# A two-block transformer kernel: order of copies and modulation blocks in the first block, who makes three low parts, and when late modulation weights are taken

## The chip, the cores and the metric

One core of a Trainium2 chip runs the whole program as one launch. The metric is device time in microseconds (us); lower is better. The kernel before took 1699.9 us, the median of 3 runs (1697.79 to 1700.61). The engines are TensorE (PE: matrix products and transposes; PEld is its weight load), VectorE (DVE), ScalarE (ACT), GpSimd (POOL) and SyncE (SP), which issues nearly all DMAs.

## The reference, cut to what matters

256 tokens of width 1024 go through a first block (a mixed attention, then a product-key expert layer) and a second block of two layers (NSA attention and MLP, then sliding-window attention with sinks and MLP). The parts that the change touches:

```python
# first block, attention
proj = h @ w_in                      # queries, keys, values, index queries/keys
ik_n = rms(ik)                       # index keys
score = sum_h(w_idx * relu(q_idx @ ik_n.T)); idx = top_k(score, 64)
x = x + g1 * (y @ w_out)             # out projection of the first block: "out1"
# experts
q = h @ w_query                      # "wq"
s = q @ sub_keys.T; i_top = top_k(s, 16)
x = x + g2 * experts(...)
# second block, two layers i = 0, 1
mod = silu(c) @ ada_w[i] + ada_b[i]  # six vectors sh1, sc1, g1, sh2, sc2, g2
y = (nsa if i == 0 else swa)(modulate(rms(x), sh1, sc1)) @ w_out   # "out2", "out3"
x = x + (1 + g1) * rms(y)
y = relu(modulate(rms(x), sh2, sc2) @ w_up)**2 @ w_down            # "mlp2", "mlp3"
x = x + (1 + g2) * rms(y)
```

## The kernel before, in words

All weight matrices are cut into chunks of 128 x 1024 float32 (512 KB) and laid out in one stream, in the order of use: `qk1` (18 chunks), `v1` (8), `out1` (8), `wq` (16), `subkeys`, `u` and `v` (128 each), `nsa`, `phi`, `out2` (8), `mlp2` (64), `swa` (10), `out3` (8), `mlp3` (64). SP loads them into a ring of 8 slots; chunk c is loaded once chunk c - 8 has been used.

Each product is made exact in three passes (`passes`, L665 to L671): a weight is split into a high part (ACT copies it to `weights_high`, L1238, 4 buffers) and a low part, weight minus high (`weights_low`, written over the ring slot). Low parts are made by POOL (`lows`, L627) or by DVE (`low`, L1711); the table `BY_DVE` says which chunk is whose. For `out1` and `out3` all are POOL's, for `out2` the first four are DVE's. The first two chunks of `wq`, `nsa`, `mlp2`, `swa` and `mlp3` are pairs with buffers of their own (`pair_high` L1242, `pair_low` L1716).

Modulation vectors are made on DVE, block by block: `ada_block` (L1662) multiplies a 128 x 1024 piece of modulation weights by the broadcast condition and sums over its columns. 144 such pieces are loaded by SP beside the stream.

Every engine runs one program written out by hand, with semaphores between them; no scheduler chooses an order. The places of the change, in order of time:

- First block, index scores: after all 18 `qk1` chunks PE transposes the index keys (L921), waits until ACT has copied them, and makes the index scores (L930), which DVE turns into a top-64 mask; then come the `v1` chunks. ACT makes the high part of the last `qk1` chunk's successor before it copies that chunk's result (`take`).
- Values: after `v1` ACT makes a high part, then copies both token tiles out of PSUM (L1397), and only then can attention use these banks (scores L801 and L811).
- First attention: 8 steps. PE: scores, transposes (L834), values (L856). ACT: exponentials, copies. DVE: maxima, scaling, low parts of y (L1791), and after each step's scaling one modulation block in steps 0 to 3 and two in steps 4 to 7; 4 more follow before `out1` ends.
- `wq` and sub-keys: PE waits for all 16 copies of `wq` results, then starts the sub-key products (L953).
- `out2` and `mlp2`: DVE takes modulation blocks 0 to 3 of the last 32, then the pair's low parts, then the residual (L2190), the norm (L1700) and so on. SP loads blocks 0 to 5 ahead; in `mlp2` DVE takes block j + 4 in step j.
- `swa`, third attention, `out3`: DVE rotates keys and queries (L2130 to L2132) while POOL makes the low parts of `out3`'s first four chunks.

Between a block's residual and its next product, PE transposes the normed tiles (L730), with `keep_busy` products (L748) between the two tiles.

## Time and profile before

| | |
|---|---|
| median of 3 runs | 1699.9 us |
| the profiled execution | 1700.1 us |
| its span in the profile | 1698.3 us |
| PE, DVE, ACT, POOL busy | 96%, 72%, 53%, 27% |
| granted TensorE clock, mean | 0.987 of full speed |
| weights moved | 344 MB, 203 GB/s |

The profile is one execution. Of the time, 1.8 us lie outside the span. "Busy" of PE is near its whole span, so what can be saved without taking work away is the little time in which it waits or runs at the lower clock.

### The profile page before, as it was taken

What the parts mean: (1) busy time and instruction counts of PE and PEld (TensorE: products, weight loads), DVE (VectorE), ACT (ScalarE), POOL (GpSimd) and SP (SyncE); (2) the same over time, 40 slices, a digit from 0 to 9 for tenths busy, and PEclk for the clock granted to TensorE, in tenths of its full rate; (3) what the DMA queues carried; (4) which work ended last, traced back from release to release, by engine and by line L of the source; (5) the groups of instructions that cost most, each with busy time, mean ns of one, the idle gap of its engine ahead of it and who ended that gap; (6) DMA issues with size and microseconds to landing.
All of it is one profiled execution on the core that took longest, in us unless ns stands there. A gap on an engine that the chain in (4) does not pass through costs nothing.

```text
span 1698.3 us, 31246 instructions
## 1 busy us (share of the span) xinstructions
PE 1635.0 (96%) x10735; PEld 1440.5 (85%) x10740; DVE 1222.5 (72%) x2382; ACT 908.2 (53%) x1747; POOL 450.5 (27%) x181
## 2 busy tenths in 40 slices
PE   6988999999999999999999999988999999799998
PEld 3975899999999999788888888965799998489997
DVE  4468869589718894877778777746598877666665
ACT  3445554455459995554554545267544445564443
POOL 0970238989875556000000000000200001020000
PEclk9999999999999999999999999999999999899999
DMA  9877776555553334888888776430488766146563
GB/s 342 303 186 238 263 231 182 184 182 178 185 173 112 113 114 134 287 285 287 285 293 295 286 258 181 152 147 1 152 298 288 275 203 159 38 150 187 186 188 106
DMA packets 105527, 344.25 MB, mean 203 GB/s; under 512 B 18484, under 2 KB 22340, under 8 KB 105445
## 3 DMA queue, kind: packets, MB, share of 16 engines
q1 hardware_dynamic: 101092, 339.19, 60.1%
q10 hardware_dynamic: 4352, 4.02, 0.8%
q8 instruction: 46, 0.75, 0.2%
q14 instruction: 37, 0.30, 0.1%
HBM read 341.02 MB, written 1.10 MB: 201 GB/s over the span
## 4 chain that ended last, share of the span: by engine, by line
PE 81%; issue 5%; POOL 4%; DVE 4%; ACT 3%; DMA 1%; ACTq 1%; SPq 0%; DVEq 0%; POOLq 0%
PE banks L669 23%; PE banks L670 23%; PE banks L671 23%; POOL weights_low L627 4%; PE banks L975 3%; PE banks L834 1%; PE banks L801 1%; PE banks L850 1%; DMA ring<-in_stream 1%; DMA arena<-in_ada 1%; ACT arena L1292 1%; PE banks L702 1%; PE banks L703 1%; PE banks L706 1%; DVE arena L2132 0%
## 5 line engine op out<-in xcount | busy, mean ns | idle before, releaser
L1238 ACT ACTIVATE weights_high<-ring 128x1024 fp32r<-128x1024 f32 x470 | 494.7, 1053 | 336.0 <-PE banks L671 324.9
L627 POOL TENSOR_TENSOR weights_low<-ring,weights_high 128x1024 fp32r<-128x1024 f32 x176 | 449.3, 2567 | 666.4 <-ACT weights_high L1238 666.1
L669 PE MATMUL banks<-ht_high,weights_high 128*128 128x256 f32 x1936 | 556.7, 288 | 3.9 <-DVE ht_low L1739 3.9
L670 PE MATMUL banks<-ht_low,weights_high 128*128 128x256 f32 x1936 | 547.8, 283 | 0.0
L671 PE MATMUL banks<-ht_high,weights_low 128*128 128x256 f32 x1936 | 547.7, 283 | 0.0
L1711 DVE TENSOR_TENSOR weights_low<-ring,weights_high 128x1024 fp32r<-128x1024 f32 x294 | 358.4, 1223 | 130.0 <-ACT weights_high L1238 129.0
L669 PEld LDWEIGHTS banks<-ht_high,weights_high 128*128 128x128 f32 x1936 | 371.1, 192 | 7.2 <-issue 4.0
L670 PEld LDWEIGHTS banks<-ht_low,weights_high 128*128 128x128 f32 x1936 | 371.4, 192 | 2.6
L671 PEld LDWEIGHTS banks<-ht_high,weights_low 128*128 128x128 f32 x1936 | 371.1, 192 | 0.0
L1662 DVE SCALAR_TENSOR_TENSOR arena<-arena,cs 128x1024 f32<-128x1024 f32 x80 | 110.1, 1386 | 47.7 <-DMA arena<-in_ada 42.8
L669 PE MATMUL banks<-weights_high,ga_parts 128*128 128x512 f32 x256 | 99.9, 390 | 2.8 <-DVE ga_parts L2039 2.8
L647 POOL MEMSET arena<- 128x1144 f32 x1 | 1.1, 1056 | 381.4 <-PE banks L671 381.4
L669 PE MATMUL banks<-weights_high,hidden_high 128*128 128x512 f32 x256 | 100.3, 392 | 0.0
L670 PE MATMUL banks<-weights_low,hidden_high 128*128 128x512 f32 x256 | 100.3, 392 | 0.0
L671 PE MATMUL banks<-weights_high,ga_parts 128*128 128x512 f32 x256 | 99.6, 389 | 0.0
L670 PE MATMUL banks<-weights_low,ga_parts 128*128 128x512 f32 x256 | 99.6, 389 | 0.0
L669 PE MATMUL banks<-weights_high,ga_more 128*128 128x512 f32 x256 | 99.6, 389 | 0.0
L670 PE MATMUL banks<-weights_low,ga_more 128*128 128x512 f32 x256 | 99.6, 389 | 0.0
L671 PE MATMUL banks<-weights_high,ga_more 128*128 128x512 f32 x256 | 99.6, 389 | 0.0
L671 PE MATMUL banks<-weights_high,hidden_low 128*128 128x512 f32 x256 | 99.6, 389 | 0.0
L2000 DVE TENSOR_TENSOR arena<-arena,banks 128x512 f32<-128x512 f32 (+1 forms) x64 | 44.0, 688 | 61.0 <-PE banks L975 55.6
L1593 ACT ACTIVATE arena<-banks 128x256 f32<-128x256 f32 x64 | 24.6, 385 | 111.5 <-PE banks L671 109.0
(274 smaller groups left out, 2589.8 us busy)
## 6 DMA issues: line engine op xcount, KB each, us to landing
ring<-in_stream SPq DMA_DIRECT2D x490, 512.0 KB, 3.5
arena<-in_ada SPq DMA_DIRECT2D x88, 512.0 KB, 5.5
ada_ring<-in_ada SPq DMA_DIRECT2D x56, 512.0 KB, 4.3
arena<-gate_store SPq DMA_DIRECT2D x5, 512.0 KB, 5.7
arena<-bias_rows ACTq DMA_DIRECT2D x1, 2048.0 KB, 20.1
X<-in_x SPq DMA_DIRECT2D x1, 1024.0 KB, 6.0
out<-X SPq DMA_DIRECT2D x4, 256.0 KB, 2.1
arena<-arena ACTq DMA_DIRECT2D x8, 127.5 KB, 4.8
```

The lines of the kernel that those rows point to most:

```text
L627: pool.tensor_tensor(WL[:, c % SLOTS, :], ring[:, c % SLOTS, :], WH[:, c % HIGHS, :], ALU.subtract)\
L669: pe.matmul(out, wh, xh, start=start, stop=False, **kw)
L670: pe.matmul(out, wh, xl, start=False, stop=False, **kw)
L671: return pe.matmul(out, wl, xh, start=False, stop=stop, **kw)
L702: pe.matmul(outs[n], wh[:, k * P:(k + 1) * P], HTH[:, k, :], start=i == 0 and n == 0, stop=False, skip_group_check=True)
L703: pe.matmul(outs[n], wl[:, k * P:(k + 1) * P], HTH[:, k, :], start=False, stop=False, skip_group_check=True)
L975: m = pe.matmul(banks[:, 2 + s, q * P:(q + 1) * P], onehot[:, s, 0, q, :], onehot[:, s, 1, q, :], start=True, stop=True)
L1238: act.activation(WH[:, c % HIGHS, :], ring[:, c % SLOTS, :], ACT.Copy).then_inc(S["high_ready"], 1)
L1593: act.activation(RELU[:, j % 2, :], out_home(o0 + j) if j < 2 else banks[:, 6 + (o0 + j) % 2, 0:T], ACT.Relu)\
L1662: dve.scalar_tensor_tensor(out=w, in0=w, scalar=1.0, in1=cs[:], op0=ALU.mult, op1=ALU.mult, accum_out=column)\
L1711: dve.tensor_tensor(WL[:, c % SLOTS, :], ring[:, c % SLOTS, :], WH[:, c % HIGHS, :], ALU.subtract)\
L2000: dve.tensor_tensor(g, g, banks[:, 2 + group % ONEHOTS, :].rearrange("p (t j) -> p j t", t=4), ALU.mult)\
```

## The change

It has five parts.

1. First block, index scores. The transposes of the index keys come after `qk1` chunk 8, and the index scores after the first `v1` chunk. `take` on ACT copies the last result of a group before it makes the next high part.
2. Values. ACT copies tile 0 of `v1`, before its high part; DVE copies tile 1 after its top-64, and step 1 of the attention waits for that (`v1_by_dve`).
3. First attention. DVE takes one modulation block in each of the 8 steps and the other 8 afterwards; between those it makes the low parts of `out1` chunks 4 to 7, which POOL made.
4. Sub-keys. PE waits for each `wq` result by itself.
5. Second block. Two of the last 32 modulation blocks come before `mlp2` instead of four, the others two steps later in it (block j + 2 in step j), and SP loads four ahead instead of six. The low parts of `out3` chunks 0 to 3 are DVE's, in the last two steps of the third attention and after it.

```diff
-BY_DVE = [FIRST_CHUNK[name] + i for name, first, n in [("qk1", 0, 2), ("wq", 2, 16), ("v", HIGHS, NKEYS), ("nsa", 2, 20), ("out2", 0, HIGHS),
-                                                    ("mlp2", 2, 64), ("swa", 2, 10), ("mlp3", 2, 64)] for i in range(first, n)]
+BY_DVE = [FIRST_CHUNK[name] + i for name, first, n in [("qk1", 0, 2), ("out1", HIGHS, 8), ("wq", 2, 16), ("v", HIGHS, NKEYS), ("nsa", 2, 20), ("out2", 0, HIGHS),
+                                                    ("mlp2", 2, 64), ("swa", 2, 10), ("out3", 0, HIGHS), ("mlp3", 2, 64)] for i in range(first, n)]
...
-            for k in (0, 2, 4):
+            for k in (0, 2):
                 load_ada_mlp(k)
                 load_ada_mlp(k + 1)
-                if k < 4:
-                    load_chunks(ahead + 2 * k, ahead + 2 * k + 4)
+                load_chunks(ahead + 2 * k, ahead + 2 * k + 4)
...
-                    load_ada_mlp(k + 6, r * DB)
+                    load_ada_mlp(k + 4, r * DB)
...
-            lows(2, chunk["wq"])
+            lows(2, chunk["out1"] + HIGHS)
...
-            lows(chunk["out3"], chunk["mlp3"])
+            lows(chunk["out3"] + HIGHS, chunk["mlp3"])
...
+                if n == 1:
+                    pe.wait_ge(S["v1_by_dve"], 1)
...
+                if m == 8:
+                    pe.wait_ge(S["ik_normed"], 2)
+                    for t in range(TT):
+                        x = pe.transpose(banks[:, 4, T + t * P:T + (t + 1) * P], IK[:, t, :], ident)
+                    x.then_inc(S["ikt_ready"], 1)
+            def index_scores(c):
+                if c:
+                    return
+                pe.wait_ge(S["ikt_taken"], 1)
+                pe.wait_ge(S["out_taken"], OUTS["qk1"] + 18)
...
-            deep("v1", 8, D)
-            pe.wait_ge(S["sel_ready"], 1)
-            pe.wait_ge(S["v1_taken"], 2)
+            deep("v1", 8, D, between=index_scores)
+            pe.wait_ge(S["v1_taken"], 1)
...
-            pe.wait_ge(S["out_taken"], OUTS["wq"] + 16)
             for t in range(TT):
                 for hp in range(16):
+                    if t == 0:
+                        pe.wait_ge(S["out_taken"], OUTS["wq"] + hp + 1)
...
-                for m in range(n):
-                    used(chunk[name] + m)
+                def copy(m):
                     pair_done(OUTS[name] + m, chunk[name])
                     act.activation(dst(m), out_home(OUTS[name] + m), func, scale=scale(m)).then_inc(S["out_taken"], 1)
+                for m in range(n - 1):
+                    used(chunk[name] + m)
+                    copy(m)
                     between(m)
+                used(chunk[name] + n - 1, None, lambda: copy(n - 1))
...
-            for t in range(TT):
-                act.activation(V1[:, t, :], banks[:, 2 * t:2 * t + 2, :].rearrange("p a b -> p (a b)"), ACT.Copy)\
-                    .then_inc(S["v1_taken"], 1)
+            used(chunk["v1"] + 7, None, lambda: act.activation(V1[:, 0, :], banks[:, 0:2, :].rearrange("p a b -> p (a b)"), ACT.Copy)
+                 .then_inc(S["v1_taken"], 1))
...
-                for k in ([step] if step < 4 else [2 * step - 4, 2 * step - 3]):
-                    ada_mixer1(k)
+                ada_mixer1(step)
+            dve.wait_ge(S["chunk_used"], chunk["v1"] + 8)
+            dve.tensor_copy(V1[:, 1, :], banks[:, 2:4, :].rearrange("p a b -> p (a b)")).then_inc(S["v1_by_dve"], 1)
...
-            for k in range(4, DB):
+            for k in range(DB):
                 ada_mixer1(DB + k)
+                if k % 2:
+                    low(chunk["out1"] + HIGHS + k // 2)
...
-                        ada_mlp(j + 4, r)
+                        ada_mlp(j + 2, r)
...
             for i in range(2):
-                ada_mlp(i)
-            for i in range(2, 4):
                 ada_mlp(i)
...
-            attention(att3)
+            def beside_att3(step):
+                if step >= len(att3) - 2:
+                    low(chunk["out3"] + step - (len(att3) - 2))
+            attention(att3, beside_att3)
+            for i in range(2, HIGHS):
+                low(chunk["out3"] + i)
```

In the rows below, `arena` is the large work buffer (here modulation weights, values, index keys), `ring` the weight ring, `ht_high` and `ht_low` the activations' parts. Helper lines shift by one on PE and by ten on DVE between the two kernels.

PE, end of `qk1` and start of `v1`, before: last `qk1` passes, transposes, index scores, first `v1` passes.

```order
L669 MATMUL banks<-ht_high,weights_high 128x256
L670 MATMUL banks<-ht_low,weights_high 128x256
L671 MATMUL banks<-ht_high,weights_low 128x256
L921 MATMUL banks<-const,arena 128x128 x2
L930 MATMUL banks<-arena 128x128 x4
L930 MATMUL banks<-arena 128x256 x4
L669 MATMUL banks<-weights_high,ht_high 128x512
```

The same engine now, end of the first `v1` chunk:

```order
L668 MATMUL banks<-weights_high,ht_high 128x512
L669 MATMUL banks<-weights_low,ht_high 128x512
L670 MATMUL banks<-weights_high,ht_low 128x512
L935 MATMUL banks<-arena 128x128 x4
L935 MATMUL banks<-arena 128x256 x4
L668 MATMUL banks<-weights_high,ht_high 128x512
```

The eight score products stand behind a whole `v1` chunk, and the two transposes have gone far ahead of them.

DVE, from the last scaling of the first attention to the residual, before (L1662 modulation blocks, L1791 low parts of y, L1716 the pair, L1896 the residual's first products):

```order
L1784 TENSOR_SCALAR arena<-arena,rsum 128x256 x4
L1662 SCALAR_TENSOR_TENSOR arena,mod<-arena,cs 128x1024 x2
L1791 TENSOR_TENSOR ht_low<-banks,ht_high 128x2x128 x3
L1662 SCALAR_TENSOR_TENSOR arena,mod<-arena,cs 128x1024 x4
L1669 TENSOR_TENSOR mod<-mod,ada_b 128x16
L1690 SCALAR_TENSOR_TENSOR scl<-mod,norms 128x8
L1716 TENSOR_TENSOR weights_low<-ring,pair_high 128x1024 x2
L1896 TENSOR_TENSOR banks<-banks,arena 128x512 x2
```

Now (L1672 modulation blocks, L1721 low parts of `out1`, L1726 the pair):

```order
L1672 SCALAR_TENSOR_TENSOR arena,mod<-arena,cs 128x1024
L1801 TENSOR_TENSOR ht_low<-banks,ht_high 128x2x128 x3
L1672 SCALAR_TENSOR_TENSOR arena,mod<-arena,cs 128x1024 x2
L1721 TENSOR_TENSOR weights_low<-ring,weights_high 128x1024
L1672 SCALAR_TENSOR_TENSOR arena,mod<-arena,cs 128x1024 x2
L1721 TENSOR_TENSOR weights_low<-ring,weights_high 128x1024
L1672 SCALAR_TENSOR_TENSOR arena,mod<-arena,cs 128x1024 x2
L1721 TENSOR_TENSOR weights_low<-ring,weights_high 128x1024
L1672 SCALAR_TENSOR_TENSOR arena,mod<-arena,cs 128x1024 x2
L1721 TENSOR_TENSOR weights_low<-ring,weights_high 128x1024
L1679 TENSOR_TENSOR mod<-mod,ada_b 128x16
```

Four blocks after the attention have become eight, and four low parts stand among them.

DVE, between the second attention and the residual before `mlp2`, before:

```order
L1711 TENSOR_TENSOR weights_low<-ring,weights_high 128x1024 x2
L1662 SCALAR_TENSOR_TENSOR arena,mod<-arena,cs 128x1024 x4
L1716 TENSOR_TENSOR weights_low<-ring,pair_high 128x1024 x2
L2190 TENSOR_TENSOR arena<-banks,arena 128x512 x2
L2195 RECIPROCAL small<-small 128x1
```

Now:

```order
L1721 TENSOR_TENSOR weights_low<-ring,weights_high 128x1024 x2
L1672 SCALAR_TENSOR_TENSOR arena,mod<-arena,cs 128x1024 x2
L1726 TENSOR_TENSOR weights_low<-ring,pair_high 128x1024 x2
L2203 TENSOR_TENSOR arena<-banks,arena 128x512 x2
L2208 RECIPROCAL small<-small 128x1
```

Two of the four modulation blocks ahead of the pair are gone from here.

## Rows read from the trace of the kernel before

**Rows 1.** The page: busy time of each engine, and the chain that ended last.

```profile
PE 1635.0 (96%) x10735; PEld 1440.5 (85%) x10740; DVE 1222.5 (72%) x2382; ACT 908.2 (53%) x1747; POOL 450.5 (27%) x181
PE 81%; issue 5%; POOL 4%; DVE 4%; ACT 3%; DMA 1%; ACTq 1%; SPq 0%; DVEq 0%; POOLq 0%
```

**Rows 2.** Waits of PE, whole span: line, what for, us, times, longest.

```profile
PE banks L753 <- DVE csilu L1816: 7.3, 1, 7.3
...
PE banks L953 <- ACT arena L1281: 1.4, 1, 1.4
```

**Rows 3.** Timeline, PE, index scores: start, us, line, operation, [idle before <- releaser].

```profile
94.22 0.38 PE L921 MATMUL banks<-const,arena 128*128 128x128 f32 x2
96.08 1.58 PE L930 MATMUL banks<-arena 64*128 64x128 f32 x16 [1.47 <-ACT arena L1387]
```

**Rows 4.** Timeline, PE, start of the first attention.

```profile
122.67 0.91 PE L801 MATMUL banks<-arena 64*128 64x128 f32 x8 [3.02 <-issue]
123.51 2.07 PE L811 MATMUL banks<-arena 128*128 128x256 f32 x4
...
129.59 1.13 PE L811 MATMUL banks<-arena 128*128 128x256 f32 x4
```

**Rows 5.** Timeline, ACT, the copies of the values.

```profile
120.66 1.92 ACT L1397 ACTIVATE arena<-banks 128x1024 f32<-128x1024 f32 x2
```

**Rows 6.** Busy time in a stretch; its last three: granted clock, DMA share, GB/s.

```profile
123.00:126.00 3.00, 3.00 (x14) 1.95 (x12) 0.38 (x1) 0.88 (x1) 0.17 (x1) 0.51 0.99 378
```

**Rows 7.** Timeline, DVE, the top-64: its mask of tile 0.

```profile
105.14 1.84 DVE L1880 TENSOR_SCALAR arena<-arena 128x128 bf16<-128x128 f32 x1
```

**Rows 8.** Timeline, PE, last step of the first attention.

```profile
162.05 1.09 PE L856 MATMUL banks<-arena 128*64 128x128 f32 x16 [1.62 <-DVE ht_low L1791]
```

**Rows 9.** Timeline, DVE, beside out1.

```profile
163.94 1.22 DVE L1662 SCALAR_TENSOR_TENSOR arena<-arena,cs 128x1024 f32<-128x1024 f32 x1
...
175.37 4.54 DVE L1716 TENSOR_TENSOR weights_low<-ring,pair_high 128x1024 fp32r<-128x1024 f32 x2
179.94 1.32 DVE L1896 TENSOR_TENSOR banks<-banks,arena 128x512 f32<-128x512 f32 x2
```

**Rows 10.** The page, costliest groups: low parts made by DVE.

```profile
L1711 DVE TENSOR_TENSOR weights_low<-ring,weights_high 128x1024 fp32r<-128x1024 f32 x294 | 358.4, 1223 | 130.0 <-ACT weights_high L1238 129.0
```

**Rows 11.** Timeline, from out2 to mlp2: SP's queue, DVE and PE.

```profile
1201.44 0.91 SPq L475 DMA_DIRECT2D arena<-in_ada  x2
...
1205.99 1.23 DVE L1662 SCALAR_TENSOR_TENSOR arena<-arena,cs 128x1024 f32<-128x1024 f32 x1 [11.71 <-DMA arena<-in_ada]
...
1210.66 1.28 DVE L2190 TENSOR_TENSOR arena<-banks,arena 128x512 f32<-128x512 f32 x2
...
1215.60 1.97 PE L730 MATMUL banks<-const,arena 128*128 128x128 f32 x8 [3.67 <-DVE arena L1700]
...
1221.93 1.04 PE L730 MATMUL banks<-const,arena 128*128 128x128 f32 x8
```

**Rows 12.** Timeline, PE, from out3 to mlp3.

```profile
1505.57 1.09 PE L730 MATMUL banks<-const,arena 128*128 128x128 f32 x8
...
1511.07 1.09 PE L730 MATMUL banks<-const,arena 128*128 128x128 f32 x8 [0.52 <-DVE arena L1700]
```

**Rows 13.** Timeline, swa into the third attention: DVE rotations, PE scores.

```profile
1431.91 0.43 DVE L2132 TENSOR_TENSOR arena<-arena 128x256 f32<-128x256 f32 x1
...
1445.30 2.35 DVE L2132 TENSOR_TENSOR arena<-arena 128x256 f32<-128x256 f32 x1
...
1447.79 1.22 PE L801 MATMUL banks<-arena 64*128 64x128 f32 x8 [1.82 <-DVE arena L2132]
...
1450.44 2.08 PE L801 MATMUL banks<-arena 64*128 64x256 f32 x8 [0.88 <-DVE arena L2132]
```

**Rows 14.** mlp2: DVE's idle time in one step, and landings.

```profile
1376.66 1.23 DVE L1711 TENSOR_TENSOR weights_low<-ring,weights_high 128x1024 fp32r<-128x1024 f32 x1 [0.99 <-ACT weights_high L1238]
...
arena<-in_ada SPq DMA_DIRECT2D x26, 512.0 KB, 4.3
```

More of the change, by code:

```diff
@@ L755, in broadcast_c, with deep @@
                 m.then_inc(S["c_rows_ready"], 1)
-            def deep(name, chunks, cols, per=1, ready=None, y=None, bank=0):
+            def deep(name, chunks, cols, per=1, ready=None, y=None, bank=0, between=lambda c: None):
                 lead = LEAD if y is not None else 0
@@ L770, in deep @@
                     m.then_inc(S["chunk_used"], 1)
+                    between(c)
                 for t in range(TT if lead else 0):
@@ L918, in _ @@
                 chunk_blocks(chunk["qk1"] + m, out_bank(OUTS["qk1"] + m), h_rhs)
-            pe.wait_ge(S["ik_normed"], 2)
-            for t in range(TT):
-                m = pe.transpose(banks[:, 4, T + t * P:T + (t + 1) * P], IK[:, t, :], ident)
-            m.then_inc(S["ikt_ready"], 1)
-            pe.wait_ge(S["ikt_taken"], 1)
-            pe.wait_ge(S["out_taken"], OUTS["qk1"] + 18)
-            for t in range(TT):
-                w = P * (t + 1)
-                for h in range(4):
-                    m = pe.matmul(rel(t, h), QK[half[h % 2], 16 + h // 2, tile[t]], IKT[half[h % 2], 0:w],
-                                  start=True, stop=True)
-                m.then_inc(S["index_ready"], 1)
-            deep("v1", 8, D)
-            pe.wait_ge(S["sel_ready"], 1)
-            pe.wait_ge(S["v1_taken"], 2)
+                if m == 8:
[8 more added lines that the diff above has]
+                pe.wait_ge(S["out_taken"], OUTS["qk1"] + 18)
+                for t in range(TT):
+                    w = P * (t + 1)
+                    for h in range(4):
+                        m = pe.matmul(rel(t, h), QK[half[h % 2], 16 + h // 2, tile[t]], IKT[half[h % 2], 0:w],
+                                      start=True, stop=True)
+                    m.then_inc(S["index_ready"], 1)
+            deep("v1", 8, D, between=index_scores)
+            pe.wait_ge(S["v1_taken"], 1)
             pe.wait_ge(S["bias_loaded"], 16)
@@ L1372, in index_keys @@
             def index_keys(m):
+                if m == 8:
+                    act.wait_ge(S["ikt_ready"], 1)
+                    act.activation(IKT, banks[:, 4, T:2 * T], ACT.Copy).then_inc(S["ikt_taken"], 1)
                 if m != 1:
@@ L1385, in _ @@
             take("qk1", 18, lambda m: QK[:, m, :], scale=lambda m: 0.125 if m < 4 or 8 <= m < 12 else 1.0, between=index_keys)
-            act.wait_ge(S["ikt_ready"], 1)
-            act.activation(IKT, banks[:, 4, T:2 * T], ACT.Copy).then_inc(S["ikt_taken"], 1)
+            used(chunk["v1"])
             act.wait_ge(S["index_ready"], 1)
```

14 lines of the change are left out of this document (8 added, 6 removed).

## The prediction, made before the change was run

> **What bounds the kernel now.** I read the page's busy shares and its chain first. PE is busy in 96% of the span and makes up 81% of the chain [rows 1]. The change takes no product away, so it can only win where PE waits or runs at the lower clock. The second view is PE's list of waits. Its longest entry, 7.3 us in the first microseconds of the program [rows 2], is not touched. The rest are short waits at the seams between stages, and the timeline of PE at each seam shows which instruction waits and for whom. Three seams lie in the first block, one at the start of `mlp2`, one at the start of the third attention. I go through them in order of time. The profiled execution took 1700.1 us, 1.8 us more than its span; the median is 1699.9 us, so what is summed here is taken from 1700.1 and moved by 0.2 us at the end.
>
> **The change, part by part.**
>
> *Index scores.* PE ends the transposes of the index keys and is idle for 1.47 us until ACT's copy is there [rows 3]. With the transposes ahead (0.2 to 0.4 us of PE there instead of here) and the scores behind a chunk of `v1`, both inputs are old when PE comes to them, so the idle time goes: 1.5 us. Behind this PE could meet POOL's low parts, but these keep pace: a low part is started as soon as ACT has made the high part four chunks ahead. DVE's top-64 starts one `v1` chunk less the idle time later against the program's start, about 0.8 us.
>
> *Values.* PE waits 3.02 us before the first attention scores [rows 4]; ACT makes a high part and then the two copies, 1.92 us [rows 5], which end as PE starts. Now one copy of 0.96 us and no high part stand there: some 1.1 us of idle time. Gain 1.9 us. The other tile is DVE's. It is needed only by step 1, behind the 0.91 + 2.07 us of step 0's scores. DVE ended its top-64 1.7 us ahead of the last `v1` product before; with `v1` 1.5 us earlier and top-64 0.8 us later it ends 0.6 us behind it. The trace has no such copy by DVE. From below it costs nothing, from above twice the 1.2 us that DVE takes for 1024 columns [rows 10], should POOL hold it up as in the mask of tile 0, 1.84 us for 128 columns [rows 7]. I take 1.2 us, the nearest. It then ends some 1.8 us behind `v1`, before step 1 wants it (2.8 us behind, at full clock); with 2.4 us it still just fits. So zero, at most 0.5 us lost.
>
> The Trainium skill (SBUF — State Buffer, "SBUF: two separate sides") says that VectorE and GpSimd take turns on one pair of SBUF ports, and that on VectorE's side only an instruction with two SBUF inputs or in a two-port mode takes it. By that rule the copy out of PSUM is never held up, since its one input is in PSUM, and the lower bound of this gain would be 1.9 us and not 1.4. No row here shows such a copy beside POOL; the mask's does show an instruction with one SBUF input held up, which the rule allows for a two-port mode.
>
> *Clock.* After the 3.02 us of idle time PE ran at a granted 0.51, the lower of its two levels (1.2 against 2.4 GHz), for 3 us [rows 6]. The four bias products took 2.07 us there and 1.13 us later [rows 4]; with the two score groups the stretch lost 1.6 us. With 1.1 us of idle time I expect the full clock: waits of 1.0 to 1.6 us at the end of the same attention left it at 1.00. Gain 1.6 us; bounds 0 and 1.8.
>
> *Tail of the attention.* In steps 5 to 7 PE has no more scores to fill its waits. DVE carries two modulation blocks a step, and the last value product waits 1.62 us for a low part queued behind them [rows 8]. With one block a step (1.15 us less in each) the scaling of step 7 is bound by ACT's exponentials. PE's last products then start 1.4 us earlier: value products of step 6 0.4 us, transposes of step 7 0.8 us, value products of step 7 1.4 us. Bounds 0.5 and 2.
>
> *`out1` on DVE.* Let T be the start of `out1` on PE (163.1 before). DVE's first block after the attention starts at T + 0.9 [rows 9]. Before, it had 4 blocks, two small instructions and the pair, but POOL's four low parts stretched them (the pair took 4.54 us [rows 9], where two free ones would take 2.3), and the residual started at 179.94 [rows 9], T + 16.9. Now it is 8 blocks and 4 low parts at 1.14 us each, 13.7 us, with 0.9 us of waiting for the first high part: T + 15.5. PE wants the last low part at T + 15.0, but POOL had also been late by 0.5 us there, so PE loses nothing new. With the pair, the residual starts at T + 18.3, 1.5 us later. Of that, 0.8 us are hidden, since the second tile's residual waited for PE before. Cost 0.7 us; bounds 0 and 2.5. The upper bound is for SP's queue: the last two loads of modulation weights now wait for DVE until T + 3.2, and the first residual's gate rows, 8 further loads and `wq`'s pair stand behind them. At 1.3 us each (512 KB at about 400 GB/s) the second of the pair lands near T + 15, and its low part is due at T + 17.
>
> *Sub-keys.* PE waited 1.4 us for the last copy [rows 2]. The first 15 results are old, and the last is wanted 1.7 us later, so this goes: 1.35 us.
>
> *Before `mlp2`.* Here DVE waited 11.71 us for modulation weights that SP issued only at 1201.44, then did two blocks and the pair, and started the residual at 1210.66 [rows 11]. The second tile's transposes came at 1221.93, 6.3 us after the first tile's, which had themselves waited 3.67 us and then ran at the lower clock [rows 11]. Blocks 2 and 3 are gone from here. The seam from `out3` to `mlp3` has the same instructions and no such blocks: there the first transposes follow the products at once and the second come 5.5 us later [rows 12]. Laid on this seam, first transposes at 1212.0 and second at 1217.5: gain 4.4 us. POOL's last low part may be stretched by the pair, as in `out3`, where it cost PE 0.5 us; bounds 3.5 and 4.7. In `mlp2` itself two more blocks stand at steps 28 and 29, in which DVE idles 0.99 us behind each low part of such a step [rows 14] and another 1 us before its next square: covered. If that cover were gone, 2.3 us.
>
> *Third attention.* DVE's 256-column additions take 0.43 us alone and 2.35 us beside POOL [rows 13]. Three of them, and one product, are stretched, and PE waits 1.82 and 0.88 us and starts scores 1 at 1450.44 [rows 13] at half clock. Without POOL the last rotation ends 1.15 us after its matmul of 1445.27, at 1447.1: scores 1 start 3.3 us earlier, and at full clock they and their masks take 1.7 instead of 3.1 us. From there the old distances hold. I take 4.5 us; bounds 2.5 (clock falls all the same) and 6. The four low parts on DVE cost 4 x 1.2 us [rows 10]. In steps 6 and 7 they lie where DVE waited 1.5 us and 2.2 us, and the last two end well before PE's third `out3` chunk. Zero.
>
> Sum: 1.5 + 1.9 + 1.6 + 1.4 - 0.7 + 1.35 + 4.4 + 4.5 = 15.95, taken as 16 us. 1700.1 - 16 = 1684.1, less 0.2: 1684 us. With all lower bounds (1.3, 1.4, 0, 0.5, -2.5, 1.2, 3.5, 2.5) it is 7.9 us, 1692; with the upper ones (1.6, 2, 1.8, 2, 0, 1.4, 4.7, 6) 19.5 us, 1680.
>
> **The rivals.**
>
> *The clock falls elsewhere.* Small waits stay at the seams, and in the profile waits of about 1.5 us were followed once by the full clock and once by half. If the gain of 1.6 us does not come, the third attention starts at half clock (2 us less), and one more stretch of 3 us runs at half (1.5 us): 16 - 5 = 11 us, 1689. For it: the moved work shifts every seam. Against: more waits vanish than arise.
>
> *DVE is too full beside `out1`.* The pair's chunk lands late, the second high part and with it DVE's pair and residual move by 3 us or more, and nearly all of the first block's gain of 7 us is halved: 1688. For it: the DMA queue is behind DVE there. Against: 2 us of slack by the count above.
>
> *More than forecast.* Half-clock stretches that I left alone, in the second attention, come out at full clock in the new alignment: 3 us more or beyond, 1681 to 1677.
>
> *Slower.* In `mlp2` the weights of a block may be loaded only when the block two before it has been taken. If the landing time (4.3 us at the median [rows 14]) grew by more than the slack of about 7 us before the block is due two steps later, DVE would wait in every step, and PE with it. 1 us over in 28 steps is 28 us: 1712. It decides from a landing of some 11 us on. Against: the kernel before had the same two buffers and the same distance there.
>
> *It gives nothing back.* The gains at one seam turn up as waits at the next, within 0.2%.
>
> **How the numbers follow.** Forecast 62%, its own range 1681 to 1687. Clock 14%, `out1` 9%, more than forecast 9%, nothing 3%, slower 3%. A range of 1679 to 1692 leaves out the last two and the far ends. A measurement can tell 0.2% (3.4 us) from no change. Faster 94%, same 3%, slower 3%.
>
> **What would show it.** Index scores without idle time; a first score group 1.1 us behind `v1` and at full clock; the last value products no longer waiting 1.6 us; the residual before `wq` at T + 18; the two transposes before `mlp2` 5.5 us apart and the first without a wait; additions of 0.43 us in the whole of `swa`, and scores 1 about 1.2 us behind scores 0. It is wrong if DVE waits for modulation weights in `mlp2`, if the residual before `wq` comes after T + 20, or if PE's clock is low where the waits have gone.

## The result, and the profile after

The changed kernel takes **1690.67 us** (median of 7 runs, 1685.92 to 1693.08) against 1699.9 before (7 runs, 1697.79 to 1702.66). The ratio is **0.9938, 95% interval 0.9928 to 0.9948**: 10.5 us faster by the ratio, 9.2 by the two medians. 1684 was forecast. A second set of five runs (a0_again below) gave 0.9935 (0.9922 to 0.9947). The profiled execution took 1689.56 us, its span 1687.3.

The page after, busy times, clock by slices, the chain, and the group of VectorE's low parts:

```profile
PE 1635.1 (97%) x10740; PEld 1442.0 (85%) x10740; DVE 1217.6 (72%) x2391; ACT 907.0 (54%) x1746; POOL 427.6 (25%) x173
PEclk8999999999999999999999999989999999999999
PE 89%; ACT 4%; DVE 3%; issue 2%; DMA 1%; ACTq 1%; POOL 0%; POOLq 0%; SPq 0%; DVEq 0%
...
L1721 DVE TENSOR_TENSOR weights_low<-ring,weights_high 128x1024 fp32r<-128x1024 f32 x302 | 368.1, 1223 | 132.6 <-ACT weights_high L1243 131.6
```

PE is busy for 1635 us as in [rows 1], so in the net all that was won was idle: stretches at half clock went in some places and came in others. The 8 low parts that moved show as 302 against 294 of [rows 10], at the same 1223 ns.

**Start of the first attention.** PE, DVE and PE again:

```profile
98.10 1.58 PE L935 MATMUL banks<-arena 64*128 64x128 f32 x16
...
119.91 1.22 DVE L1899 COPY arena<-banks 128x1024 f32<-128x1024 f32 x1
...
120.06 0.72 PE L803 MATMUL banks<-arena 64*128 64x128 f32 x8 [1.11 <-ACT arena L1407]
120.70 1.13 PE L813 MATMUL banks<-arena 128*128 128x256 f32 x4
```

The index scores carry no bracket now: 1.47 us of [rows 3] are gone. The first scores wait 1.11 us instead of 3.02 [rows 4] and their bias products take 1.13 us instead of 2.07, which is full clock. The copy on DVE took 1.22 us, where 1.2 was guessed.

**From the attention to `wq`.** The attention ends at T = 157.8 (163.1 before). SP's queue, ACT, DVE and PE behind it:

```profile
161.34 0.43 SPq L510 DMA_DIRECT2D arena<-gate_store  x1
161.81 0.91 SPq L529 DMA_DIRECT2D arena<-in_ada  x2
162.76 0.55 SPq L467 DMA_DIRECT2D ring<-in_stream  x1
...
164.59 0.70 SPq L467 DMA_DIRECT2D ring<-in_stream  x1
...
171.91 1.06 ACT L1247 ACTIVATE pair_high<-ring 128x1024 fp32r<-128x1024 f32 x1 [4.66 <-DMA ring<-in_stream]
172.88 1.04 ACT L1243 ACTIVATE weights_high<-ring 128x1024 fp32r<-128x1024 f32 x1
177.03 1.06 ACT L1247 ACTIVATE pair_high<-ring 128x1024 fp32r<-128x1024 f32 x1 [3.12 <-DMA ring<-in_stream]
...
173.95 1.23 DVE L1721 TENSOR_TENSOR weights_low<-ring,weights_high 128x1024 fp32r<-128x1024 f32 x1 [1.73 <-ACT weights_high L1243]
...
178.12 1.23 DVE L1726 TENSOR_TENSOR weights_low<-ring,pair_high 128x1024 fp32r<-128x1024 f32 x1 [1.52 <-ACT pair_high L1247]
179.26 1.29 DVE L1907 TENSOR_TENSOR banks<-banks,arena 128x512 f32<-128x512 f32 x2
...
175.23 0.50 PE L668 MATMUL banks<-weights_high,ht_high 128*128 128x512 f32 x1 [2.27 <-DVE weights_low L1721]
...
188.42 1.09 PE L729 MATMUL banks<-const,arena 128*128 128x128 f32 x8 [0.58 <-DVE arena L1710]
```

Read it from the bottom up. The second tile's transposes come at T + 30.7 (190.05 before, T + 26.9). The residual started at 179.26, T + 21.5, and it stood behind DVE's low part of the second `wq` chunk, that behind ACT's high part, that behind a load. The same chain, one chunk earlier, holds PE: the first `wq` chunk was issued at 162.76 and taken at 171.91, 9 us later; ACT waited for it 4.66 us with the high part of the *last `out1` chunk* queued behind (172.88); DVE's low part (173.95) and PE (175.23) follow. Behind the wait of 2.27 us the clock fell as well: from 176.7 to 180.2 the products of `out1` took 0.63 us instead of 0.39, about 1.7 us in all. Of the 5.4 us that the attention's earlier end gave, 1.6 are left at 188.42.

**Before `mlp2`, and the third attention.** PE and DVE, and, as the last line, the stretch in which the clock was low before (PE busy, granted clock, the DMA engines' share, GB/s):

```profile
1211.33 1.09 PE L729 MATMUL banks<-const,arena 128*128 128x128 f32 x8
...
1216.83 1.09 PE L729 MATMUL banks<-const,arena 128*128 128x128 f32 x8 [0.52 <-DVE arena L1710]
...
1360.39 1.23 DVE L1721 TENSOR_TENSOR weights_low<-ring,weights_high 128x1024 fp32r<-128x1024 f32 x1 [0.99 <-ACT weights_high L1243]
...
1436.78 0.43 DVE L2145 TENSOR_TENSOR arena<-arena 128x256 f32<-128x256 f32 x1
1440.08 0.42 DVE L2145 TENSOR_TENSOR arena<-arena 128x256 f32<-128x256 f32 x1
...
1440.86 0.72 PE L803 MATMUL banks<-arena 64*128 64x128 f32 x8
...
1442.34 1.13 PE L803 MATMUL banks<-arena 64*128 64x256 f32 x8 [0.43 <-DVE arena L2145]
...
1440.00:1462.00 22.00, 18.15 (x133) 1.00 0.22 71
```

The transposes are 5.50 us apart and the first have no wait, where [rows 11] had 3.67 us and half clock. In `mlp2` DVE waits for ACT's high part as in [rows 14], never for modulation weights. The additions take 0.43 us where [rows 13] had 2.35, and the seam runs at full clock (1.00, where the same stretch before has 0.77).

### The profile page after: what moved, and what is told of

Same layout as the page of the kernel before. It is cut to its first block, busy times and chain, and to the rows that moved or that the text cites. A ratio compares the mean times of both kernels' runs of the same rounds, so it can differ in the third digit from the quotient of the medians.

```text
span 1687.3 us, 31233 instructions
## 1 busy us (share of the span) xinstructions
PE 1635.1 (97%) x10740; PEld 1442.0 (85%) x10740; DVE 1217.6 (72%) x2391; ACT 907.0 (54%) x1746; POOL 427.6 (25%) x173
## 4 chain that ended last, share of the span: by engine, by line
PE 89%; ACT 4%; DVE 3%; issue 2%; DMA 1%; ACTq 1%; POOL 0%; POOLq 0%; SPq 0%; DVEq 0%
PE banks L668 25%; PE banks L669 25%; PE banks L670 25%; PE banks L980 3%; PE banks L836 2%; DMA ring<-in_stream 1%; PE banks L803 1%; ACT arena L1301 1%; PE banks L852 1%; ACT weights_high L1243 1%; PE banks L813 1%; PE banks L701 1%; PE banks L705 1%; PE banks L702 1%; DVE arena L1794 1%
## 5 line engine op out<-in xcount | busy, mean ns | idle before, releaser
L626 POOL TENSOR_TENSOR weights_low<-ring,weights_high 128x1024 fp32r<-128x1024 f32 x168 | 426.4, 2548 | 678.3 <-ACT weights_high L1243 678.0
L1721 DVE TENSOR_TENSOR weights_low<-ring,weights_high 128x1024 fp32r<-128x1024 f32 x302 | 368.1, 1223 | 132.6 <-ACT weights_high L1243 131.6
L1672 DVE SCALAR_TENSOR_TENSOR arena<-arena,cs 128x1024 f32<-128x1024 f32 x80 | 106.6, 1341 | 36.4 <-DMA arena<-in_ada 31.3
```

The costliest lines, as they stand in the source:

```text
L626: pool.tensor_tensor(WL[:, c % SLOTS, :], ring[:, c % SLOTS, :], WH[:, c % HIGHS, :], ALU.subtract)\
L1672: dve.scalar_tensor_tensor(out=w, in0=w, scalar=1.0, in1=cs[:], op0=ALU.mult, op1=ALU.mult, accum_out=column)\
L1721: dve.tensor_tensor(WL[:, c % SLOTS, :], ring[:, c % SLOTS, :], WH[:, c % HIGHS, :], ALU.subtract)\
```

## The experiments

The same fixed instructions on PE were timed in the traces of before, after and the experiments. *Attention start* is PE's first attention scores; *T* the end of its last value product; *norm* the second tile's transposes; the last column runs from the second transposes before `swa` to the first before `mlp3`. From the second `mlp3` transposes to the span's end all took 192.7 or 192.8 us.

| trace | start to attention start | to T | T to norm before `wq` | to second norm before `nsa` | to second norm before `mlp2` | `swa` to `mlp3` |
|---|---|---|---|---|---|---|
| before | 122.7 | 40.5 | 26.9 | 841.1 | 190.8 | 96.8 |
| after | 120.1 | 37.7 | 30.7 | 840.2 | 188.2 | 90.8 |
| a0_again | 118.4 | 37.7 | 30.7 | 842.4 | 188.1 | 90.7 |
| e1_act | 120.0 | 37.7 | 31.2 | 840.3 | 185.2 | 90.8 |
| e2_act_sp | 119.4 | 37.7 | 27.3 | 840.2 | 187.4 | 90.8 |
| e3_pool | 120.3 | 37.7 | 33.1 | 840.0 | 188.6 | 92.1 |
| b_mlp2 | 123.9 | 39.8 | 28.0 | 841.0 | 186.8 | 96.2 |
| b_out3 | 122.2 | 40.5 | 26.9 | 843.2 | 192.4 | 90.7 |
| b_front | 120.7 | 39.6 | 27.4 | 839.9 | 192.4 | 96.7 |
| b_out1 | 123.8 | 39.3 | 30.9 | 841.5 | 191.0 | 95.2 |
| b_fill4 | 122.6 | 40.5 | 26.9 | 841.1 | 190.9 | 93.7 |
| e4_fill | 119.9 | 37.7 | 27.2 | 840.2 | 182.3 | 90.7 |
| e5_fills | 120.1 | 37.7 | 27.3 | 840.2 | 183.6 | 92.3 |
| a_no_out3 | 119.5 | 37.7 | 30.6 | 840.3 | 185.4 | 96.8 |

### The changed kernel again: a0_again

No edit.

> The changed kernel once more, unaltered, for its spread and a second trace. All theories: 1690.7 within 3 us, ratio to the kernel before 0.993 to 0.996. Theory C (the granted clock falls at some seams in one run and not in the next, and this makes the 7 us between its fastest and slowest run): in the second trace the stretch of half clock at the second attention's start (1122 to 1132.5 in the first trace, 2.5 us longer than before) or the one at the program's start has another length, and seams with no idle time read the same within 0.3 us. Theory against it: the same lengths again, so that the change itself causes them.

Measured: 1690.05 us (1688.42 to 1692.99), ratio 0.9935 (0.9922 to 0.9947). The second attention started at half clock for as long as in the first trace, so this one of theory C's two signs did not come. But the program's start took 1.7 us less, with a granted clock of 0.69 from 33 to 44 us where the first trace has 0.53, which is C's other sign; and this stretch, in the middle of the expert layer, was low where the first trace had full clock:

```profile
679.00:683.00 4.00, 4.00 (x12) 0.57 0.45 181
```

It is the busy time, the granted clock and the DMA columns of a stretch of 4 us in which PE was never idle. Just before, PE had waited 2.0 us for `ga_parts`, where the first trace has 1.5. Together the two cost 2.2 us (842.4 against 840.2 in the table), some 1.7 of it the clock. Single traces of one kernel thus differ by some 2 us in one segment.

### ScalarE's order alone: e1_act

```diff
                 for c in range(DB - LEAD):
                     used(chunk[name] + c)
-                    if c >= 2:
+                    if c >= 2 and name != "out1":
                         pair_high(chunk[name] + DB + c - 2)
+                if name == "out1":
+                    for c in range(2):
+                        pair_high(chunk[name] + DB + c)
```

> The changed kernel with ScalarE making the upper part of the output projection's last chunk before those of the first two query chunks. Theory A (the seam behind the first attention is late because the loads of the first two query chunks land late, at 171.9 and 177.0, and ScalarE waits for the first of them with the last chunk's upper part queued behind it): TensorE's wait of 2.3 us for VectorE's lower part of the last chunk goes, but VectorE's residual still waits behind the lower part of the second query chunk, whose load lands at 177.0, so that it starts at 179.3 as before and the first transposes of the norm stay at 183.9: time within 1 us of the changed kernel's. Theory B (VectorE's own 8 blocks and 4 lower parts are the bound): the wait stays above 1 us. Theory D (TensorE's wait is what makes the seam late, the residual following from it): the transposes come 2.3 to 3 us earlier and so does the end, 1688.

Measured: 1689.67 us, ratio 0.9933 (0.9917 to 0.995): no different from the changed kernel. ACT, DVE and PE:

```profile
168.90 1.07 ACT L1243 ACTIVATE weights_high<-ring 128x1024 fp32r<-128x1024 f32 x1 [1.66 <-PE banks L670]
...
176.89 1.06 ACT L1247 ACTIVATE pair_high<-ring 128x1024 fp32r<-128x1024 f32 x1 [3.56 <-DMA ring<-in_stream]
...
177.99 1.23 DVE L1729 TENSOR_TENSOR weights_low<-ring,pair_high 128x1024 fp32r<-128x1024 f32 x1 [3.23 <-ACT pair_high L1247]
179.13 1.29 DVE L1910 TENSOR_TENSOR banks<-banks,arena 128x512 f32<-128x512 f32 x2
...
173.39 0.50 PE L668 MATMUL banks<-weights_high,ht_high 128*128 128x512 f32 x1 [0.45 <-DVE weights_low L1724]
...
183.81 0.48 PE L729 MATMUL banks<-const,arena 128*128 128x128 f32 x1 [3.30 <-DVE arena L1713]
```

The last high part now comes at 168.90 and PE waits 0.45 us instead of 2.27. The residual has not moved (179.13 against 179.26), DVE idles 3.23 us ahead of the pair's second low part, and the norm comes at T + 31.2. PE ends `out1` sooner and then waits 3.30 us for the first norm (183.81, against 183.94 without a wait in the changed kernel). Theory A held, and D fell: PE's wait was visible in the list of waits and removing it alone gave nothing, since DVE's chain through the residual ended as late. It was a near tie: in a0_again and a_no_out3 the residual starts at T + 20.9 and T + 20.7, and the second tile's part of it waits 0.5 to 0.6 us for PE, so there PE's chain ended last. B has DVE without a pause, and that it had not.

### With SyncE's order: e2_act_sp

```diff
             sp.wait_ge(S["values_done"], len(att1))
+            for i in range(2):
+                load_chunk(chunk["wq"] + i)
             for k in range(8):
                 load_ada_wq(k)
-                if k % 2:
-                    load_chunk(chunk["wq"] + k // 2)
+                if k % 4 == 3:
+                    load_chunk(chunk["wq"] + 2 + k // 4)
```

and e1_act's edit.

> As e1_act, and SyncE issues the loads of the first two query chunks ahead of the eight late modulation loads (behind the gate row). Theory A: they are issued at about 162 and 163.6 and land by 168 and 170; the residual starts 18.3 us behind the attention's end, about 176.0 instead of 179.3, and the kernel is 3.3 us faster than the changed one (3.0 to 4.0): about 1687.4, ratio to the kernel before 0.9925. Theory B: under 1 us faster, and VectorE works without a pause from 158.6 to the residual, which still starts after 178.

Measured: **1684.76 us** (1682.0 to 1688.19), ratio **0.9907 (0.9893 to 0.9921)**. SP, ACT, DVE and PE:

```profile
161.27 1.95 SPq L467 DMA_DIRECT2D ring<-in_stream  x2
...
168.34 1.06 ACT L1245 ACTIVATE weights_high<-ring 128x1024 fp32r<-128x1024 f32 x1 [1.66 <-PE banks L672]
169.31 2.06 ACT L1249 ACTIVATE pair_high<-ring 128x1024 fp32r<-128x1024 f32 x2
...
172.98 2.35 DVE L1731 TENSOR_TENSOR weights_low<-ring,pair_high 128x1024 fp32r<-128x1024 f32 x2
175.25 1.29 DVE L1912 TENSOR_TENSOR banks<-banks,arena 128x512 f32<-128x512 f32 x2
...
184.40 1.09 PE L731 MATMUL banks<-const,arena 128*128 128x128 f32 x8 [0.57 <-DVE arena L1715]
```

ACT no longer waits for a load. The residual starts at T + 18.1 (the prediction's T + 18.3) and the norm comes at T + 27.3, 3.4 us sooner than in the changed kernel. Theory A stands: what e2_act_sp adds to e1_act is the place of two loads in SP's queue, and with it the seam's delay goes. DVE's work, theory B, fills the time up to T + 18.1 and no more. The loads' new place with ACT's old order was not run, so whether e1_act's edit is needed for these 3.4 us is open. The time fell by 5 us where 3.3 were expected; the 1.7 over lie within the intervals of the two ratios.

### GpSimd makes the low parts again: e3_pool

```diff
-BY_DVE = [... ("qk1", 0, 2), ("out1", HIGHS, 8), ("wq", 2, 16), ...
+BY_DVE = [... ("qk1", 0, 2), ("wq", 2, 16), ...
-            lows(2, chunk["out1"] + HIGHS)
+            lows(2, chunk["wq"])
-                if k % 2:
-                    low(chunk["out1"] + HIGHS + k // 2)
```

> The changed kernel with the lower parts of the output projection's second four chunks made by GpSimd as before the change, all else kept. Theory A: the last upper part still comes at 172.9, GpSimd's subtraction takes 2.4 us against VectorE's 1.2, so that TensorE's wait grows from 2.3 to about 3.5 us; the residual still waits for the query chunk that lands at 177: within 1 us of the changed kernel, rather slower. Theory B: VectorE has 4.9 us less to do, the residual starts 2 to 3 us earlier and the kernel is as much faster.

Measured: 1692.21 us, ratio 0.9939 (0.9922 to 0.9956). PE:

```profile
177.19 0.80 PE L668 MATMUL banks<-weights_high,ht_high 128*128 128x512 f32 x1 [3.96 <-POOL weights_low L626]
```

The wait grew to 3.96 us, and the norm came at T + 33.1, 2.4 us later than in the changed kernel: behind the same late high part, GpSimd is the slower maker (2.4 us for a low part against DVE's 1.2), and the clock fell behind the wait. The residual still started at 179.35, T + 21.3: DVE's 4.9 us less of work gained nothing. B fell a second time. The delay of the norm does not show in the time; the two ratios' intervals overlap.

### One part at a time on the kernel before

**b_mlp2** (modulation blocks of the second MLP alone: `for k in (0, 2, 4)` to `(0, 2)`, `load_ada_mlp(k + 6)` to `(k + 4)`, `ada_mlp(j + 4, r)` to `(j + 2, r)`, blocks 2 and 3 out of the seam).

> The kernel before with only the edit of the modulation blocks before and in the second MLP. Theory A (each seam's gain is what the two traces show between the same instructions): TensorE's wait of 3.67 us before the norm's transposes goes, with the half clock behind it, 4.2 us faster, ratio 0.9975. Rival: the blocks put into the MLP's loop make VectorE late there, TensorE waits in the loop and the gain is under 2 us.

Measured: 1696.76 us, ratio 0.9974 (0.9962 to 0.9986). As expected by A.

**b_out3** (`("out3", 0, HIGHS)` into `BY_DVE`, GpSimd's `lows` from the fifth chunk, DVE's from the last two steps on).

> The kernel before with only the third attention's part: VectorE makes the lower parts of the third output projection's first four chunks, so that GpSimd is idle beside the rotary additions. Theory A (the stretches of half clock from 1447.7 to 1454.2 and from 1457.8 to 1461 came from TensorE's wait of 1.82 and 0.88 us on those additions): all of it goes, 6.0 us faster, ratio 0.9965. Rival (the clock's fall there was a matter of the run): only the waits go, 2.3 us, ratio 0.9985 or above.

Measured: 1697.67 us, ratio 0.9989 (0.9977 to 1.0). The segment fell by 6.0 us as A has it, to 90.7, but the time by some 2 (by the ratio) to 3 (by the medians, 1700.83 of before). The ratio is the rival's (0.9985 or above), the segment is A's, and the rival's reason, that the fall there was a matter of the run, does not hold: all five traces with neither this part nor dummy products have one at this seam. In the trace of b_out3 the other segments took back some of the 6.0 us: 2.1 in the expert layer, where the clock fell to 0.57 from 682 to 686, and 1.6 up to `mlp2`.

**b_front** (index keys, index scores, values' copy on DVE, sub-keys' waits).

> The kernel before with only the first block's part that leaves the modulation blocks and the output projection alone: index keys turned early, index scores between the value chunks, the copy of the second half of the values on VectorE, the sub-keys' waits one by one. Theory A: 1.5 + 1.9 + 1.6 + 1.35 = 6.3 us faster, ratio 0.9963. Rival (a part of it is lost where the residual waits for something that does not move with it, as in the changed kernel): the attention ends 5 us earlier but the norm's second transposes only 2 or 3 us, and the kernel is 3 to 4 us faster.

Measured: 1697.11 us, ratio 0.9977 (0.9967 to 0.9986), 3.9 us. The attention started 2.0 us sooner than in the trace of before (3.2 on average over the table), the sub-keys gave 1.2. What is short of A is the clock. The stretch in which it fell moved and did not go; around the attention's start, and some 38 us later:

```profile
119.00:123.00 4.00, 2.89 (x21) 1.00 0.95 150
158.00:162.00 4.00, 3.54 (x20) 0.58 0.42 155
```

In b_mlp2 the same happened without any edit in this place: PE waited its 3.0 us, the clock stayed at 1.00 at 123 to 127 and fell to 0.57 at 159 to 167.

**b_out1** (one modulation block in each attention step, eight and four low parts on DVE beside `out1`).

> The kernel before with only one modulation block in each attention step, the other eight beside the output projection, and the projection's last lower parts on VectorE. Theory A (SyncE issues the last modulation loads late, so the first query chunks land late): the attention ends 1.4 us earlier, the residual starts 21.6 us behind it instead of 18.8, and with TensorE's wait of 2 to 3 us the kernel is 2.3 us slower than the one before, ratio 1.0013. Rival (the collision needs the earlier start of the attention that the other edits give): no slower than before, rather 1 us faster.

Measured: **1703.71 us, ratio 1.0013 (0.9999 to 1.0026)**. PE and DVE at the seam, T = 163.1:

```profile
180.61 0.50 PE L669 MATMUL banks<-weights_high,ht_high 128*128 128x512 f32 x1 [2.28 <-DVE weights_low L1711]
...
183.76 1.23 DVE L1716 TENSOR_TENSOR weights_low<-ring,pair_high 128x1024 fp32r<-128x1024 f32 x1 [1.79 <-ACT pair_high L1242]
184.91 1.29 DVE L1895 TENSOR_TENSOR banks<-banks,arena 128x512 f32<-128x512 f32 x2
```

Wait and residual (T + 21.8; T + 16.8 before, where the expectation has 18.8) are those of the changed kernel, so the collision is this part's own. Taken alone, it is the one part that does not make the kernel faster. The four ratios multiply to 0.9953; the changed kernel has 0.9935 and 0.9938. With an uncertainty of 0.001 in each the difference says little. In the attention itself the front alone took 39.6 us, this part alone 39.3, and both 37.7 in each of eight traces. But b_front and b_out1 each have a stretch at half clock that begins inside the attention (158.6 and 125.1), and the eight traces have none, so this need not be more than the clock.

### Wait and clock taken apart: b_fill4

```diff
                 if kind == "swa":
+                    if n < att3[0]["n"] + 2:
+                        keep_busy(8 if n == att3[0]["n"] else 4, 4)
                     pe.wait_ge(S["rope_done"], ROPE2 + ROPE3 - (2 if n == att3[0]["n"] else 0))
```

> The kernel before with eight dummy products ahead of TensorE's wait for the third attention's first scores and four ahead of the second's; the waits for VectorE's rotary additions stay. It parts the wait from the clock. Theory A (the half clock at this seam, 10.2 us of it in the trace of before, follows TensorE's idle 1.8 and 0.9 us): the stretches of half clock at 1447 to 1462 go, the waits end as before, the stretch from swa's second transposes to those before the third MLP falls from 96.2 (95.2 to 96.8 in four traces) to about 93, and the kernel is 3 us faster, ratio 0.998. Theory C (a fall that is prevented in one place comes in another): the stretch falls but the kernel's time does not, under 1.5 us.

Measured: 1699.25 us, ratio 0.9984 (0.9973 to 0.9994). PE, and the stretch (clock in the third column from the end):

```profile
1446.05 1.67 PE L748 MATMUL banks<-const,ident_b 128*128 128x512 bf16 x7
1447.73 0.71 PE L803 MATMUL banks<-arena 64*128 64x128 f32 x8
...
1448.61 1.03 PE L748 MATMUL banks<-const,ident_b 128*128 128x512 bf16 x4
1450.38 1.13 PE L803 MATMUL banks<-arena 64*128 64x256 f32 x8 [0.75 <-DVE arena L2134]
...
1440.00:1462.00 22.00, 17.88 (x124) 1.00 0.32 101
```

Both score groups start at the same microsecond as in [rows 13], but at full clock (0.71 and 1.13 us against 1.22 and 2.08), and the segment falls from 96.8 to 93.7: some 3 us of the 6.0 were the clock, the other 3 the waits. The ratio says 2.7 us.

### Filling the second attention's wait: e4_fill and e5_fills

```diff
                 if kind == "cmp":
+                    if g == 0 and t == 0:
+                        keep_busy(10, 2 * (n % 2))
                     pe.wait_ge(S["cmp_taken"], 6)
```

> e2_act_sp with ten dummy products ahead of TensorE's wait of 2.4 us for the compressed keys in the second attention. Theory A (that idle time is what lets the clock fall there, for 6.8 us in two traces and 10.2 in eight): the half clock behind it goes, 2 to 4 us faster than e2_act_sp, about 1682, ratio to the kernel before 0.989. Theory C: the fall comes elsewhere in the second attention and the time is within 1 us of e2_act_sp.

Measured: **1680.86 us** (4 runs, 1680.13 to 1684.85), ratio **0.9879 (0.9861 to 0.9898)**, the fastest of all. The stretches at the second attention's start and end, first in e2_act_sp, then in e4_fill:

```profile
1117.00:1122.00 5.00, 2.65 (x13) 0.53 0.05 19
1122.00:1133.00 11.00, 10.14 (x79) 0.90 0.00 0
1172.00:1186.00 14.00, 11.41 (x44) 0.51 0.00 0
```

```profile
1117.00:1122.00 5.00, 4.84 (x22) 0.66 0.18 70
1122.00:1133.00 11.00, 9.80 (x85) 1.00 0.00 1
1172.00:1191.00 19.00, 16.35 (x87) 1.00 0.25 83
```

The size is as expected, the place only in part. (Half clock at this place lasted 6.8 us in three traces and 10.2 in seven, not in two and eight as the expectation has it.) PE is busy through the wait, yet the clock still fell at first (0.66), and the second pair of value products starts only 0.5 us sooner than without the fill, counted from the norm before `nsa`. At this clock the ten products took 3.7 us and outlasted the wait by 1.3. The full clock came at the attention's *end*, 50 us later, where PE's waits are the same 1.1 us as ever. In this one trace both together are worth 5 us. By the medians e4_fill is 3.9 us faster than e2_act_sp, but the intervals of their ratios overlap a little, so the gain is likely and not certain.

e5_fills adds, in each attention, behind its last two transposes:

```diff
                     probs_transpose(s)
+                    if i >= len(steps) - 2:
+                        keep_busy(5, 2 * (s["n"] % 2))
```

> e4_fill with five dummy products behind each of the last two transposes of probabilities of each of the three attentions, where TensorE waits 1.1 us for ScalarE's copies. Theory A: the half clock at the second attention's end (1172 to 1191, 6.8 to 13.6 us of it) gets shorter, 2 us faster than e4_fill, about 1680. Theory C: no faster than e4_fill; the dummy products, 1.1 us apiece of five, may make the steps later by 0.1 to 0.5 us.

Measured: 1683.13 us (4 runs), ratio 0.9888 (0.987 to 0.9906). No faster than e4_fill, as C had it. Its trace has full clock at the second attention's start, but 0.57 from 1169 to 1177 and from 1439 to 1443, where that of e4_fill has 1.00.

### The changed kernel without its third part: a_no_out3

b_out3's edit taken out of the changed kernel.

> The changed kernel without its part in the third attention (GpSimd again makes all lower parts of the third output projection, beside the rotary additions). In single traces this part is worth 5.2 us between fixed instructions (swa's second transposes to those before the third MLP: 96.2 against 91.0 on average), but alone on the kernel before it gave a ratio of 0.9989, some 2 us. Theory A (the traces' 5.2 us is its worth): ratio to the kernel before 0.9967 to 0.9970 against the changed kernel's 0.9935 and 0.9938. Theory C (part of what full clock gives at this seam is lost again elsewhere on average): ratio 0.995 to 0.996, a worth of 2 to 3.5 us.

Measured: 1693.81 us, ratio 0.9958 (0.9944 to 0.9972). Against 0.9935 and 0.9938 the part is worth some 3.6 us. The ratio lies in C's range (0.995 to 0.996), and A's 0.9967 to 0.9970 lies inside the interval too, so this run favours C and does not exclude A. The segment went back to 96.8.

## Why the prediction was right, and where it was off

The direction and the range held: 1690.67 lies between 1679 and 1692. The forecast of 1684 was 6.7 us too low and its own range (1681 to 1687) missed by 3.7, for two reasons that stood among the rivals. By steps, forecast against the difference of the table's means with and without each part (e5_fills is left out of all rows; the two traces with a fall of the clock inside the expert layer out of the sub-keys' row, e1 to e4 out of the row of `out1`, e4 out of that before `mlp2`, b_fill4 out of the third attention's):

| step | forecast | traces | |
|---|---|---|---|
| index scores and values | 1.5 + 1.9 | 3.2 | right |
| clock at the attention, its tail | 1.6 + 1.4 | 2.6 | right in sum |
| `out1` and residual | -0.7 | **-3.5** | wrong |
| sub-keys | 1.35 | 1.0 | right |
| before `mlp2` | 4.4 | 4.4 | right |
| third attention | 4.5 | 5.4 | size low |
| sum | 15.95 | 13.1 | |

**The step that failed is the cost of `out1` on DVE,** 0.7 us with an upper bound of 2.5, where the traces have 3.5. By the prediction's own sign this term is wrong: the residual before `wq` was to come at T + 18 and not after T + 20, and it came at T + 21.5. That the sum stayed inside its range is owed to the range's width, and to the other steps, which came out near their forecasts.

Within this term the arrival of `wq`'s pair was mis-sized. The prediction has SP's last load of modulation weights held until T + 3.2, which is what happened (160.97), counts 1.3 us for each load from there on, and so puts the pair's second chunk near T + 15 and its low part at T + 17. ACT took this chunk at T + 19.3 (177.03). The spacing was nearly right: most of the loads behind landed 1.3 us after the one before, with the DMA engines' share at 1.00 and 413 GB/s from 168 to 180. But the load issued at 160.97 landed 5.0 us later (one issued alone at 155.58 took 3.5), and the seven landings behind it, up to the pair's second chunk, took 11.0 us, 1.6 each (2.0 for the gate rows). So a load's own time to landing was left out, and the spacing was somewhat short: the pair's chunks landed 9.1 and 12.4 us after their issue.

A second thing was left out and cost nothing alone: ACT works in order, and its high part of the *first* `wq` chunk stands ahead of that of the last `out1` chunk, so that PE waited 2.27 us for a load of the next stage (e1_act).

The rival "DVE is too full beside `out1`" gave the right price (3 us or more) and, in its text, the right cause, the late chunk of the pair; only its title blames DVE. e3_pool relieves DVE and gains nothing, e2_act_sp moves two loads, with e1_act's edit, and brings the norm from T + 30.7 to T + 27.3.

**The third attention** was priced well by adding wait and clock separately (b_fill4: 3.0 and 3.0). The forecast of 4.5 us left out a part of what the clock was worth; of the eight traces with the part only those of e3_pool and e5_fills have a fall there.

**The rest is the clock, the first rival.** The traces' steps sum to 13.1 us, the ratio gives 10.5. In the trace of before the clock had fallen at 123 to 127 and for a short time at the second attention's start (6.8 us of half clock, where after, a0_again, e3_pool, b_mlp2, b_out3, b_front and b_out1 have 10.2). A forecast worked out from one execution takes the falls of that execution for the kernel's. Some are not: with the same 3.02 us wait, four traces (before, b_out3, b_out1, b_fill4) fell within 1.3 us of the attention's start, and b_mlp2's fell 35 us later. Of the third attention's 5.4 us, b_out3 and a_no_out3 showed 2 to 3.6 in time, and where the rest goes is open. No trace has a fall between this seam and `mlp3`, and nothing ahead of the seam can depend on it; unseen falls in the runs without a profile would explain it, and so would chance in the samples. The runs don't tell these apart.

The slower rival (`mlp2`'s loads) did not come: b_mlp2's loop is as long as before (`mlp2` to `swa`, 186.9 in each trace).

The prediction's rule of the Trainium skill (SBUF — State Buffer, "SBUF: two separate sides"), by which a copy out of PSUM is not held up by GpSimd, stays untested: the copy took 1.22 us at 119.91, between GpSimd's subtractions of 117.40 to 119.79 and of 121.03 on, and it fell between two of them in the same way in all nine traces that have it.

## What to carry to other kernels

When work is spread later, its loads are spread later too: list what stands behind them in the load queue, count the loads in flight ahead of each and add its own time to landing, and follow each to the in-order engine that takes it, since a late load for the next stage can hold up the present one there. A wait that an engine's list shows may cost nothing if another chain ends later at the same seam; undo one and then both before you believe either (without PE's wait the kernel was no faster, e1_act; with the loads moved too it was 5 us faster, e2_act_sp). And price each seam as wait plus clock, but expect the clock's part only on average: take it from several executions, or fill the idle time with dummy products and see.

## What the hardware showed that was not expected

- The clock's fall does not stand at a fixed place behind an idle time. After the same wait of 3.02 us it fell within 1.3 us in four traces (0.51 at 123 to 126 in that of before) and stayed at 1.00 in a fifth, b_mlp2, which fell to 0.57 at 159 to 167. In two traces, a0_again and b_out3, it fell to 0.57 (679 to 683 and 682 to 686) among back-to-back products behind a wait of 2.0 us, where the trace of after had 1.5 us and full clock.
- With ten dummy products in one wait of 2.4 us the mean granted clock of all runs was 0.994 (four runs) against 0.990 (five), and in the trace most of it came 50 us behind them.
- A load of 512 KB landed in 3.6 us at the median of the whole program's ring loads. When SP had issued fifteen such loads within 9.1 us (159.82 to 168.91), they landed one behind another, mostly 1.3 us apart, so each waited for all ahead of it: the two of the pair took 9.1 and 12.4 us, the last one 15.8.
